# Layer 0's end norm: variance taken about the mean of four tiles while the output products still run, and layer 1's first three products in one loop

## The reference

```
proj = (x * (1 + scale) + shift) @ w_in         # start of a layer: q_lat (384 columns), kv_lat (256), k_rope (32), ...
q_lat, kv_lat = rms_norm(q_lat), rms_norm(kv_lat)
...
out = m @ w_o                                   # end of a layer
x = layer_norm(ALPHA * x + gate * out, ln_g, ln_b)
```

## Time and profile before

| | us |
|---|---|
| median of 3 runs (lowest to highest) | 2220.85 (2219.37 to 2221.35) |
| the profiled execution, its own time | 2220.64 |
| its span | 2218.9 |
| PE busy | 2163.9 (98%) |
| DVE, ACT, POOL busy | 1424.1, 873.9, 1076.0 |

### The profile page before, as it was taken

The page is one execution under the profiler, slowest core; times in us unless marked ns, Lnnn a source line. Parts: engine busy times, 40 slices in busy tenths (PEclk is TensorE's granted clock), DMA queues, the critical chain, the costliest instruction groups (busy, mean ns, idle before and its releaser), DMA issues.

```text
span 2218.9 us, 31199 instructions
## 1 busy us (share of the span) xinstructions
PE 2163.9 (98%) x11368; PEld 1757.6 (79%) x11368; DVE 1424.1 (64%) x2306; ACT 873.9 (39%) x1470; POOL 1076.0 (48%) x1269
## 2 busy tenths in 40 slices
PE   8999999999999999999999999999999999999998
PEld 6777778888687777888677888887787887788886
DVE  3698858763568886987677565628576776533322
ACT  3644453222654445222353333334344344433321
POOL 3555437665355544776435443332434344344443
PEclk9999999999999999999999999999999999999999
DMA  8222227753322223765323222232424232222222
GB/s 287 88 88 84 76 82 259 247 200 115 104 95 86 77 76 111 235 208 186 105 67 108 100 92 89 93 116 100 133 69 152 96 123 91 67 76 76 77 77 76
DMA packets 97829, 259.93 MB, mean 117 GB/s; under 512 B 10638, under 2 KB 20238, under 8 KB 97564
## 3 DMA queue, kind: packets, MB, share of 16 engines
q1 hardware_dynamic: 76224, 212.51, 29.7%
q10 hardware_dynamic: 21468, 45.56, 5.7%
HBM read 237.01 MB, written 20.97 MB: 116 GB/s over the span
## 4 chain that ended last, share of the span: by engine, by line
PE 70%; issue 14%; POOL 8%; DVE 5%; ACT 2%; DMA 1%; ACTq 0%; POOLq 0%; DVEq 0%
PE bank L2250 21%; PE bank L2252 21%; PE bank L2251 21%; POOL t L493 7%; DVE t L1907 2%; PE bank L2501 2%; PE bank L2514 1%; PE bank L2525 1%; PE bank L2350 1%; DVE t L1359 1%; DMA t<-w_ada 1%; PE bank L2669 0%; DVE t L1865 0%; DVE t L1355 0%; PE bank L2366 0%
## 5 line engine op out<-in xcount | busy, mean ns | idle before, releaser
L493 POOL TENSOR_TENSOR t<-t,t 128x256 fp32r<-128x256 f32 x1168 | 995.7, 885 | 972.0 <-ACT t L586 971.7
L2250 PE MATMUL bank<-t,t 128*128 128x512 f32 x3012 | 1155.8, 384 | 13.8 <-DVE t L1355 6.0
L2251 PE MATMUL bank<-t,t 128*128 128x512 f32 x3012 | 1127.6, 374 | 0.0
L2252 PE MATMUL bank<-t,t 128*128 128x512 f32 x3012 | 1127.1, 374 | 0.0
L2250 PEld LDWEIGHTS bank<-t,t 128*128 128x128 f32 x3012 | 567.1, 188 | 142.4 <-issue 10.2
L2251 PEld LDWEIGHTS bank<-t,t 128*128 128x128 f32 x3012 | 567.4, 188 | 103.2 <-issue 4.3
L2252 PEld LDWEIGHTS bank<-t,t 128*128 128x128 f32 x3012 | 566.3, 188 | 104.3
L586 ACT ACTIVATE t<-t 128x1024 fp32r<-128x1024 f32 x302 | 317.2, 1054 | 294.9 <-PE bank L2252 261.7
L1701 DVE SCALAR_TENSOR_TENSOR t<-t,t,t 128x512 f32<-128x512 f32 x240 | 217.4, 906 | 7.7 <-ACT t L775 1.0
L1421 DVE SCALAR_TENSOR_TENSOR t<-t,t,t 128x512 f32<-128x512 f32 x168 | 160.9, 978 | 37.7 <-ACT t L872 25.4
L1359 DVE SCALAR_TENSOR_TENSOR t<-t,bank 128x512 f32<-128x512 f32 x112 | 76.7, 685 | 127.7 <-ACT t L1299 57.6
(11 more groups left out here) (277 smaller groups left out, 1669.9 us busy)
## 6 DMA issues: line engine op xcount, KB each, us to landing
t<-blocks SPq DMA_DIRECT2D x306, 512.0 KB, 3.6
t<-w_ada SPq DMA_DIRECT2D x160, 256.0 KB, 4.2
t<-w_ada SPq DMA_DIRECT2D x14, 512.0 KB, 10.1
xm_park<-t ACTq DMA_DIRECT2D x16, 384.0 KB, 2.3
s_park<-t ACTq DMA_DIRECT2D x16, 384.0 KB, 2.3
t<-xm_park ACTq DMA_DIRECT2D x16, 384.0 KB, 4.7
t<-s_park ACTq DMA_DIRECT2D x16, 384.0 KB, 5.4
xc_park<-t ACTq DMA_DIRECT2D x16, 256.0 KB, 2.0
```

The costliest lines, as they stand in the source:

```text
L493: low = pool.tensor_tensor(w_lo[slot][:, part], w_raw[slot][:, part], w_hi[slot][:, part].bitcast(F32), ALU.subtract)
L2250: pe.matmul(out, wh, xh, start=start, stop=False)
L2251: pe.matmul(out, wh, xl, start=False, stop=False)
L2252: return pe.matmul(out, wl, xh, start=False, stop=stop)
```

## The change

The variance of layer 0's end norm is no longer taken from centred tiles. When the first four r tiles are there, their sum over the partitions ("x_pivot") is made in the middle of wo chunk 4, and minus that mean is added to all tiles (`offset`): to r_0 to r_3 in place, and to the old x before r_4 to r_7 are made. ACT squares the offset tiles while the output products run, PE sums the first six squares in the middle of wo chunk 7, and the variance is the mean of the squares minus the square of the mean. The rest of the mean is taken off tile by tile in layer 1's first loop. Behind the norm, `first_chunks` does three blocks for each k in place of two; the splits of the weights, `layer_out` and `park_layer` stand at later places of ACT's list.

The pieces of the diff stand in the order of the file: the constants, ACT at the start of a layer, ACT at its end, DVE in layer 1's first loop, DVE at the end of a layer, PE.

```diff
+        x_sq_t = (tmp[0][:], tmp[1][:], tmp[4][:], tmp[2][:], prob[:, 0, :], prob[:, 1, :])
+        OFFSET = {4: (0, 1, 5), 5: (2, 3, 6), 6: (7,)}
+        SQUARES = (4, 0, 1, 5, 2, 3, 6, 7)
...
                 for j in range(3):
-                    made_ahead = l and j == 1
-                    evac(q_lat[:, j, :], banks[(0, 1, 4)[j]][:], (l, "q_lat", j), B_QL(l) + j if l and j != 1 else None)
-                    if made_ahead:
-                        for i in range(KT):
-                            layer_out(l - 1, i)
-                        split_to(B_QL(l) + j + 1 + RING)
+                    evac(q_lat[:, j, :], banks[(0, 1, 4)[j]][:], (l, "q_lat", j), None)
...
                 if l:
-                    evac(kv_lat[:, 0, :], banks[3][:], (l, "kv_lat", 0), B_KVL(l))
+                    split_to(B_QL(l) + 2 + RING)
+                    evac(kv_lat[:, 0, :], banks[3][:], (l, "kv_lat", 0), None)
...
                 if l:
-                    park_layer(l - 1)
+                    split_to(B_KVL(l) + 1 + RING)
+                    for i in range(KT):
+                        layer_out(l - 1, i)
...
                 split_to(B_KVL(l) + 2 + RING)
+                if l:
+                    park_layer(l - 1, range(3))
...
                     evac(qf[0:NOPE, h, :], banks[Q_BANK[h % 4]][0:NOPE, :], (l, "q", h), None)
+                    if l and h < KT - 3:
+                        park_layer(l - 1, (3 + h,))
...
+                def x_squares(ns):
+                    for n in ns:
+                        j = SQUARES[n]
+                        act.wait_ge(dve_done, Dn(l, "r" if j >= KT // 2 else "x_off", j))
+                        if n >= 6:
+                            act.wait_ge(pe_done, P(l, "x_sq", n - 6))
+                        act.activation(x_sq_t[n % 6], x[:, j, :], ACT.Square).then_inc(act_done, a(l, "x_sq", n))
                 for j in range(KT):
+                    if l < L1 - 1 and j in (5, 6):
+                        x_squares(range(3 * j - 15, 3 * j - 12))
+                    if l < L1 - 1 and j == KT - 1:
+                        root_ahead()
+                        x_squares((6, 7))
+                        continue
                     act.wait_ge(pe_done, P(l, "wo", j))
                     split_to(B_O(l) + j + 1 + RING)
...
                 if l < L1 - 1:
-                    root_ahead()
+                    act.wait_ge(dve_done, Dn(l, "x_var"))
+                    act.activation(tmp[2][:, 0:128], tmp[2][:, 0:128], ACT.Sqrt, bias=eps_x[:], scale=1.0 / D).then_inc(act_done, a(l, "x_std"))
+                    act.wait_ge(pe_done, P(l, "wo", KT - 1))
+                    split_to(B_O(l) + KT + RING)
+                    continue
...
                     if j < KT:
+                        wd(l - 1, "x_cent", j)
...
+                    if 0 < j < KT - 1:
+                        x_cent(l - 1, j + 1)
...
+                def offset(tiles, j):
+                    wd()
+                    dve.scalar_tensor_tensor(tiles[:, j, :], banks[6][:], -2.0 / D, tiles[:, j, :], ALU.mult, ALU.add).then_inc(dve_done, d(l, "x_off", j))
...
+                if l < L1 - 1:
+                    wp(l, "x_off_sum")
+                    dve.tensor_scalar(tmp[2][:, 0:128], banks[4][:, 0:128], -1.0 / D, None, ALU.mult).then_inc(dve_done, d())
+                    wd()
+                    dve.tensor_tensor(tmp[2][:, 0:128], tmp[2][:, 0:128], banks[4][:, 0:128], ALU.mult).then_inc(dve_done, d())
+                    wp(l, "x_sq", KT - 1)
+                    wd()
+                    dve.tensor_tensor(tmp[2][:, 0:128], tmp[2][:, 0:128], banks[3][:, 0:128], ALU.add).then_inc(dve_done, d(l, "x_var"))
+                    wa(l, "x_std")
+                    dve.reciprocal(tmp[2][:, 0:128], tmp[2][:, 0:128]).then_inc(dve_done, d(l, "x", "rstd"))
+                    wp(l, "x_mean")
+                    x_cent(l, 0)
+                    x_cent(l, 1)
+                    wp(l, "x", "spread")
+                    continue
...
                 if l:
-                    first_chunks(banks[0:2], B_QL(l), [(l, "q_lat", j) for j in range(2)], lambda k: Dn(l, "uL", k))
-                    u_chunk(banks[4], B_QL(l) + 2, (l, "q_lat", 2))
+                    first_chunks((banks[0], banks[1], banks[4]), B_QL(l), [(l, "q_lat", j) for j in range(3)], lambda k: Dn(l, "uL", k))
                     u_chunk(banks[3], B_KVL(l), (l, "kv_lat", 0))
...
+                        middle = {4: lambda: pivot_sum(l), KT - 1: lambda: x_square_sums(range(6))}.get(j)
...
+                if l < L1 - 1:
+                    pe.wait_ge(dve_done, Dn(l, "r_sum", KT - 2))
+                    sum_quarters(banks[4], tmp[3], True, False, (l, "x_off_first"))
+                    x_square_sums((6,))
+                    pe.wait_ge(dve_done, Dn(l, "r", KT - 1))
+                    sum_quarters(banks[4], x[:, KT - 1, :], False, True, (l, "x_off_sum"))
+                    x_square_sums((KT - 1,))
+                    sum_rows(banks[7], tmp[3][:], 2, 0, (l, "x_mean_first"))
+                    sum_rows(banks[7], x[:, KT - 1, :], 2, 1, (l, "x_mean"))
+                    continue
```

More of the change, by code:

```diff
@@ L667, in _, with park_layer @@
                     u_high(l, j)
-                def park_layer(l):
+                def park_layer(l, js):
                     act.wait_ge(act_done, A(l, "y", KT - 1))
-                    for j in range(KT):
+                    for j in js:
                         act.dma_start(x_park[j], x[:, j, :]).then_inc(x_parked, 16)
@@ L1530, in x_norm, with x_cent @@
                 dve.scalar_tensor_tensor(x[:, j, :], x[:, j, :], V("ln_g", l, j), banks[6][:], ALU.mult, ALU.mult).then_inc(dve_done, d(l, "x_norm", j))
+            def x_cent(l, j):
+                dve.scalar_tensor_tensor(x[:, j, :], banks[7][:], -1.0 / D, x[:, j, :], ALU.mult, ALU.add).then_inc(dve_done, d(l, "x_cent", j))
             def context_parts(js):
@@ L1846, in _ @@
                         dve.wait_ge(x_back, 16 * (KT // 2) * (l + 1))
+                        if l < L1 - 1:
+                            wp(l, "x_pivot")
+                            offset(x_old, j)
                     wp(l, "wo", j)
                     held = x if j < KT // 2 else x_old
+                    if l < L1 - 1 and j >= KT // 2:
+                        wd(l, "x_off", j)
                     dve.scalar_tensor_tensor(x[:, j, :], banks[j % 2][:], ada[:, l, 2 * KT + j:2 * KT + j + 1], held[:, j, :], ALU.mult, ALU.add)\
                         .then_inc(dve_done, d(l, "r", j))
-                    if 0 < j < KT - 1:
+                    if l < L1 - 1:
+                        if j % 4 and j < KT - 1:
+                            wd()
+                            dve.tensor_tensor(tmp[3][:], x[:, j - 1, :] if j % 4 == 1 else tmp[3][:], x[:, j, :], ALU.add).then_inc(dve_done, d(l, "r_sum", j))
+                        for i in OFFSET.get(j, ()):
+                            offset(x if i < KT // 2 else x_old, i)
+                    elif 0 < j < KT - 1:
                         wd()
@@ L2447, in _ @@
                 if l:
+                    pe.wait_ge(dve_done, Dn(l - 1, "x_norm", KT - 1))
                     u_chunk(banks[6], B_KVL(l) + 1, (l, "kv_lat", 1), turn)
@@ L2626, in _, with pivot_sum, x_square_sums @@
                                   (l, "yb", jj, k), (b,) if half else ())
+                def pivot_sum(l):
+                    pe.wait_ge(dve_done, Dn(l, "r_sum", KT // 2 - 1))
+                    sum_rows(banks[6], tmp[3][:], 1, 0, (l, "x_pivot"))
+                def x_square_sums(ns):
+                    for n in ns:
+                        pe.wait_ge(act_done, A(l, "x_sq", n))
+                        sum_quarters(banks[3], x_sq_t[n % 6], n == 0, n == KT - 1, (l, "x_sq", n))
                 pe.wait_ge(act_done, A(l, "mg", KT - 1, 2))
@@ L2631, in _ @@
                     pe.wait_ge(dve_done, Dn(l, "r", j - 2))
-                    chunk(banks[j % 2][:], [(B_O(l) + j, k, mH[:, k, :], mL[:, k, :]) for k in range(KT)], (l, "wo", j), (B_O(l) + j,))
+                    middle = None
+                    if l < L1 - 1:
+                        middle = {4: lambda: pivot_sum(l), KT - 1: lambda: x_square_sums(range(6))}.get(j)
+                    chunk(banks[j % 2][:], [(B_O(l) + j, k, mH[:, k, :], mL[:, k, :]) for k in range(KT)], (l, "wo", j), (B_O(l) + j,), middle)
                     if l == L1 - 1 and 2 <= j <= 4:
                         norm_sums(range(3 * j - 6, min(3 * j - 3, KT)), CTX, ("nc",), ctx_tmp, 4)
+                if l < L1 - 1:
+                    pe.wait_ge(dve_done, Dn(l, "r_sum", KT - 2))
[7 more added lines that the diff above has]
+                    continue
                 pe.wait_ge(dve_done, Dn(l, "r_sum", KT - 2))
```

2 lines of the change are left out of this document (added).

## The result

Nine runs of each kernel: before 2221.07 us, after 2224.83 us (2223.32 to 2228.64). The ratio is 1.0022 with a 95% interval of 1.0014 to 1.0031, so the kernel became 0.2% slower, 3.8 us by the medians and 4.9 us by the ratio. The forecast was 2226.5 within 2221.8 to 2230.0.

A forecast was written before the change was run, and what follows sets the result against it. PE, busy in 98% of the span, was taken as the bound. The terms -3.0 + 0.2 + 6.3 + 1.7 + 0.5 = +5.7 us on 2220.64 gave 2226.3, by the median 2226.5, within 2221.8 to 2230.

The forecast's parts named there:

- Part 5: Products behind the pause: PE's granted clock falls to half for 3.4 us, +1.7 us, bounds 0.7 and 3.4.
- Part 6: ACT's later lists up to kv_lat's root: moved splits, layer_out and DMA issues make the root late, +0.5 us (0 to 1.2).
- Part 4: After layer 1's first three chunks: PE waits for block 90's weights, whose slot frees late, +6.3 us (5.9 to 7.0).
- Part 1 and 2: Output products and norm's end: sums move under the products, layer 1's first product comes at 565.6 against 568.62, -3.0 us.
- (c): Rival at the seams: clock falls at the norm's end or stays low longer, DMA issues slow; +9, 2229.6 us, chance 0.15.
- Part 3: Layer 1's first loop, three chunks for each k: DVE and PE level at about 2.05 us a step, +0.2 us (0 to 1.2).
- (a): Rival at block 90: the pause comes, the clock does not fall or falls inside it; +4.0, 2224.9 us, chance 0.20.
- (b): Rival at block 90: no pause, its weights are ready in time; -2.3, 2218.6 us, chance 0.08.
- (d): Rival in the three-chunk loop: DVE becomes the bound; 2227.5 us, counted as upper part of the forecast's 0.52.

The follow-up runs named there:

- e2: The changed kernel with block 90's split on ACT moved from behind the third copy and squares to right behind the first q_lat copy; 2223.53 us, ratio 1.0009.
- e5: The changed kernel with 8 KB of its own for block 90's high and low parts, and the splits of blocks 90 and 91 earlier; 2218.40 us, ratio 0.9991.
- e4: The kernel before, keeping its old end norm, with three chunks for each k and the changed kernel's ACT order; 2229.16 us, ratio 1.0033.
- e1: The changed kernel with six filler matmuls on PE behind the three first chunks, in the pause; 2223.79 us, ratio 1.0013.
- e3: The changed kernel's new norm, but with two chunks for each k and ACT's order as in the kernel before; 2221.40 us, ratio 1.0007.
- e7: The kernel of e5 without the one filler matmul in front of the norm's spread; 2218.80 us, ratio 0.9994 to the kernel before.

## Why the prediction was right, step by step

The forecast was a sum of +5.7 us; the stage that it speaks of became 5.70 us longer. That the two agree to the last digit is luck: Part 5 was taken 0.8 too small, and Part 6 0.5 and Part 4 0.3 too large. The mechanism, a pause at block 90 and slow products behind it, came as told.

- **Part 1 and 2, -3.0 in the sum:** measured -3.10. Output chunk 4 with the pivot sum took 6.35 us and chunk 7 with the six sums of squares 7.15, for 5.44 (r_3 to r_4 and r_6 to r_7 on DVE), as told. The row sums end at 560.8, the filler at 561.7, and the first u starts at 562.8; counted from the end of the output products, the sum had these within 0.15. The unseen 128x128 adds take 0.29 us each; 0.3 was taken. The sum took filler and spread at full clock without saying so; only rival (c) has the fall of the clock at this place, and with the fall 1.2 us of the gain would have been missing.
- **Part 3, +0.2:** measured +0.30. DVE's round lasts 2.05 us, 2.06 in the prediction; six rounds are so long, not seven, since the last has no subtraction. One round of DVE, changed kernel (L1557 the subtraction, L1626 u, L1630 uL):

```profile
569.05 0.68 DVE L1557 SCALAR_TENSOR_TENSOR t<-bank,t 128x512 f32<-128x512 f32 x1
569.77 0.75 DVE L1626 SCALAR_TENSOR_TENSOR t<-t,t,bank 128x512 f32<-128x512 f32 x1
570.44 0.75 DVE L1630 SCALAR_TENSOR_TENSOR t<-t,t,t 128x512 fp32r<-128x512 f32 x1
```

  The wait in front of u costs, as the earlier trace rows had it: u starts 0.72 us behind a subtraction of 0.68, while uL starts 0.67 us behind a u of 0.75, and the next subtraction (571.10) 0.66 behind a uL of 0.75. By the Trainium skill's rule that a semaphore between two DVE instructions is free (VectorE: DVE Perf Modes, "The DRAIN you can't avoid") u would start as early behind its predecessor as the other two do; this trace does not agree (0.04 behind its end, where they start before it).
- **Part 4, +6.3:** measured 6.03, 3.14 after moving only the split (e2), none with an own slot (e5). This is the step on which the whole rests; e2 and e5 show it, and e4 shows the same pause without the new norm.
- **Part 5, +1.7:** mis-sized; 2.5 by the products' length and 2.3 by e1. The spell of lower clock lasted 6.7 us, about twice the 3.4 at the program's start: 1.9 in the pause and 4.8 on products, where the sum had 3.4. The cost stays within the bound of 3.4. Behind e2's pause of 3.14 us the products had 3.1 to 3.4 us of it.
- **Part 6, +0.5:** wrong. What failed is that the DMA issues of the parking were counted as ACT time. They stand in ACT's list, but in this trace they run beside its computations. The copy of kv_lat's second chunk came 0.18 us late (8.00 us behind q_lat's sums for 7.82), not 0.4 to 0.5, and the slack in front of kv_lat's root took that up. ACT's timeline, changed kernel:

```profile
604.38 0.63 ACT L689 ACTIVATE t<-t 128x512 f32<-128x512 f32 x1
604.62 0.34 ACTq L675 DMA_DIRECT2D x_park<-t  x1
604.90 0.62 ACT L689 ACTIVATE t<-t 128x512 f32<-128x512 f32 x1
604.98 0.68 ACTq L675 DMA_DIRECT2D x_park<-t  x1
...
609.06 0.69 ACT L722 ACTIVATE t<-bank,t 128x512 f32<-128x512 f32 x1 [1.03 <-PE bank L2415]
```

  kv_lat's root waits 1.03 us for PE, for 1.20 before: ACT is still ahead. From q_lat's sums to the score product both kernels take 46.71 us.
- **The rivals:** (a), no fall of the clock or one that lies inside the pause, did not come in either profile, though 1.9 us of the spell lay there; e1 shows what it would have given. (b) is what e5 had to be built for. Of (c) a part came, the longer spell, and its +9 did not: the clock is at 1.00 at the norm's end, and the DMA issues cost nothing. Its 2229.6 is counted from the profiled execution; from the median, as the others are, it is 2229.9. (d) is out: DVE's round was 2.05 us, and the pause came in e4 too, without a subtraction in the loop.
- **From the stage to the whole:** the median moved by 3.8 us in the first set and 7.0 in the second, the ratios by 4.9 and 7.1. The stage's 5.7 lies between. The reason for the spread in profiles is the clock's spells elsewhere; that it is also the reason in the unprofiled runs is inferred, from mean clocks of 0.994 in the shortest runs of the changed kernel (2223.3) and 0.991 in the longest (2228.5).

## What to carry to other kernels

Where several products are woven into one loop to hide a slow producer, count the weight slots: all of them are held until the last round, so the next block's preparation can't be hidden and stands behind whatever the preparing engine has in its list. Here a slot more took the whole cost away (stage 101.75, e5). The split placed early took away half of the pause, which was not enough: 106.20 (e2) against 105.30 with two chunks for each k (e3). When a change touches some 100 us of a long program whose clock wavers elsewhere, compare the stage between two fixed instructions, and leave the medians to say only whether it matters.

## What was not expected of the hardware

- A low part on POOL slows some DVE instructions beside it and not others. In the changed kernel the first uL (564.29) took 0.75 us, with POOL idle from 563.57. In e5 the low part of block 90 runs there, and the uL took 1.20. DVE and POOL of e5:

```profile
564.41 1.20 DVE L1639 SCALAR_TENSOR_TENSOR t<-t,t,t 128x512 fp32r<-128x512 f32 x1
565.54 0.68 DVE L1566 SCALAR_TENSOR_TENSOR t<-bank,t 128x512 f32<-128x512 f32 x1
```

```profile
563.64 3.27 POOL L544 TENSOR_TENSOR t<-t,t 128x256 fp32r<-128x256 f32 x4
```

  In e7 two uL meet it, and both are slow; the u between them, which reads a PSUM bank, is not. DVE and POOL of e7:

```profile
564.64 1.22 DVE L1639 SCALAR_TENSOR_TENSOR t<-t,t,t 128x512 fp32r<-128x512 f32 x1
566.50 0.75 DVE L1635 SCALAR_TENSOR_TENSOR t<-t,t,bank 128x512 f32<-128x512 f32 x1
567.17 1.24 DVE L1639 SCALAR_TENSOR_TENSOR t<-t,t,t 128x512 fp32r<-128x512 f32 x1
```

```profile
564.58 3.28 POOL L544 TENSOR_TENSOR t<-t,t 128x256 fp32r<-128x256 f32 x4
```

  The whole trace of the kernel before shows the same: of its scalar_tensor_tensor of 128x512 without an operand in a bank (t<-t,t,t, rows of a single instruction) the 28 that run wholly beside POOL's work took 1.02 to 1.30 us, and the 28 that run with POOL idle 0.74 to 0.75. With one operand in a bank (t<-bank,t,t) the 15 wholly beside POOL took 0.74 to 0.75, as alone. In e5 the slower uL delayed the first product by 0.45 us (0.95 of waiting for 0.50); without it e5's stage would be 101.3, an estimate.
- Identical code had half clock for 3.5, 7 or 10 us at layer 1's end in different executions, and what lies behind the stage took 1578.9 to 1582.5 us in the ten profiles. In front of it r_3 started between 532.63 and 535.22 us.
